# The chunks of a SwiGLU product transposed by DMA on 16-bit halves instead of by TensorE

## What is computed

```python
D_FF = 2816
for l in range(DEPTH):                      # DEPTH = 2
    ...                                     # the mixer: x = x + merged @ w_out[l]
    h2 = rms_norm(x, norm_ffn[l])
    x = x + (jax.nn.silu(h2 @ w_ffn_gate[l]) * (h2 @ w_ffn_up[l])) @ w_ffn_down[l]
```

## Time and profile before

| | |
|---|---|
| median of 3 executions | 848.45 us (848.27 to 849.31) |
| the profiled execution, device time | 849.7 us |
| its span in the profile | 847.9 us |
| granted TensorE clock over the span | 0.999 of full speed |
| PE / DVE / ACT / POOL busy | 842.3 / 552.7 / 420.1 / 69.2 us |

### The profile page before, as it was taken

How to read it: one execution, slowest core, us unless ns; L and a number is a source line. 1 busy time by engine, 2 the same in 40 slices (tenths; PEclk the granted TensorE clock), 3 DMA queues, 4 the chain that set the end, 5 groups by cost and what they waited for, 6 DMA issues and landing times.

```text
span 847.9 us, 10500 instructions
## 1 busy us (share of the span) xinstructions
PE 842.3 (99%) x4100; PEld 689.4 (81%) x4100; DVE 552.7 (65%) x688; ACT 420.1 (50%) x505; POOL 69.2 (8%) x86
## 2 busy tenths in 40 slices
PE   9999999999999999999999999999999999999998
PEld 7888778888888888888888877778888888888886
DVE  5999565657775656654379984565686666656552
ACT  6766544564354444443456665544744544444330
POOL 1333000000030000000024310000000200000000
PEclk9999999999999999999999999999999999999999
DMA  9745334444546555555455543444445555545551
GB/s 351 269 166 192 130 132 174 162 143 157 197 167 226 199 175 175 195 194 187 172 192 199 180 168 106 168 162 148 163 155 194 193 179 192 192 169 186 198 190 59
DMA packets 23116, 151.60 MB, mean 179 GB/s; under 512 B 2816, under 2 KB 2976, under 8 KB 5664
## 3 DMA queue, kind: packets, MB, share of 16 engines
q1 hardware_dynamic: 21152, 144.71, 48.3%
q0 software_dynamic: 1632, 6.18, 2.0%
q10 hardware_dynamic: 288, 0.08, 0.0%
HBM read 149.91 MB, written 1.05 MB: 178 GB/s over the span
## 4 chain that ended last, share of the span: by engine, by line
PE 98%; ACT 1%; DMA 0%; DVE 0%; SPq 0%; issue 0%
PE bank L917 30%; PE bank L919 29%; PE bank L928 29%; PE bank L950 5%; PE bank L1057 2%; PE bank L1033 1%; PE bank L1024 1%; PE bank L997 1%; DMA x_sb<-in_x_dram 0%; PE bank L1003 0%; DVE w_lo L643 0%; PE bank L1067 0%; ACT w_hi L499 0%; ACT zvu L610 0%; ACT aT_hi L509 0%; ACT probsT L521 0%
## 5 line engine op out<-in xcount | busy, mean ns | idle before, releaser
L643 DVE TENSOR_TENSOR w_lo<-w_raw,w_hi 128x2048 fp32r<-128x2048 f32 x134 | 307.0, 2293 | 128.3 <-ACT w_hi L499 128.0
L917 PE MATMUL bank<-w_hi,aT_hi 128*128 128x512 f32 x832 | 333.3, 401 | 0.0
L919 PE MATMUL bank<-w_hi,aT_lo 128*128 128x512 f32 x832 | 325.0, 391 | 0.0
L499 ACT ACTIVATE w_hi<-w_raw 128x2048 fp32r<-128x2048 f32 x134 | 256.1, 1913 | 100.3 <-DMA w_raw<-in_stream_dram 100.1
L928 PE MATMUL bank<-w_lo,aT_hi 128*128 128x512 f32 x832 | 223.7, 391 | 0.1
L917 PEld LDWEIGHTS bank<-w_hi,aT_hi 128*128 128x128 f32 x832 | 156.6, 188 | 36.0 <-issue 5.0
L928 PEld LDWEIGHTS bank<-w_lo,aT_hi 128*128 128x128 f32 x832 | 155.6, 188 | 33.4 <-DVE w_lo L643 0.6
L919 PEld LDWEIGHTS bank<-w_hi,aT_lo 128*128 128x128 f32 x832 | 156.7, 188 | 30.7
L917 PE MATMUL bank<-w_hi,hT_hi 128*128 128x512 f32 x176 | 68.9, 391 | 0.0
L919 PE MATMUL bank<-w_hi,hT_lo 128*128 128x512 f32 x176 | 68.5, 389 | 0.0
L514 ACT ACTIVATE hT_hi<-bank 128x512 fp32r<-128x512 f32 x22 | 13.2, 598 | 78.1 <-PE bank L950 78.1
(11 more groups left out here) (97 smaller groups left out, 717.6 us busy)
## 6 DMA issues: line engine op xcount, KB each, us to landing
w_raw<-in_stream_dram SPq DMA_DIRECT2D x135, 1024.0 KB, 4.7
bias_sb<-in_b_gate_dram POOLq DMA_DIRECT2D x12, 256.0 KB, 4.5
par<-in_params_dram POOLq DMA_DIRECT2D x3, 384.0 KB, 3.5
w_raw<-in_stream_dram SPq DMA_DIRECT2D x4, 256.0 KB, 4.9
pool_mat<-in_pooling_dram POOLq DMA_DIRECT2D x1, 1024.0 KB, 8.2
out_dram<-x_sb SPq DMA_DIRECT2D x4, 256.0 KB, 4.0
x_sb<-in_x_dram SPq DMA_DIRECT2D x2, 256.0 KB, 4.0
x_sb<-in_x_dram SPq DMA_DIRECT2D x1, 512.0 KB, 6.2
```

Source lines behind the costliest of these rows:

```text
L499: nc.scalar.activation(w_hi[:, j % RING, :, :].rearrange("p k n -> p (k n)"), w_raw[:, j % RING, :, :].rearrange("p k n -> p (k n)"), ACT. ...
L643: nc.vector.tensor_tensor(w[0], w[1], w[2].bitcast(F32), ALU.subtract).then_inc(unit_lo, 1)
L917: nc.tensor.matmul(o, src[0][:, k, tok], w_hi[:, slot, wk + i, :], start=first and i == 0, stop=False)
L919: nc.tensor.matmul(o, src[1][:, k, tok], w_hi[:, slot, wk + i, :], start=False, stop=False)
```

## The change

The four PE transposes of each `hid` chunk go, with their PSUM bank. In their place:

- GpSimd, `hidden_halves`: two copies that take the low and the high 16 bits of every float32 of `hid` (all 512 elements of a partition) to `halves`.
- SP, `turn_hidden`: one transposing DMA of 128 x 1024 16-bit elements, `halves` to `turned`, issued right behind the load of a weight unit. Its place is counted from `unit_done`: chunk i is issued when unit `U_FFN` + 2i + 2 is done, and after `halves_ready`. SP's hardware loop over units is written out in Python so that this can stand between two loads.
- GpSimd, `hidden_whole`: two copies that put the halves together again in `hT_raw` (float32, the transposed chunk). GpSimd does halves of i, whole of i, halves of i + 1, and so on.
- ACT and DVE take `hT_hi` and `hT_lo` from `hT_raw` in SBUF, in their step `U_FFN` + 2i + 5, two units later than before. `hT_raw` lies on the memory of `hT_lo`; `halves` and `turned` lie on that of `qkT`.
- PE's matmuls of the down projection wait for `hidden_ready`, which DVE raises.

The PSUM banks 6 and 7 are dealt out to the remaining turns in the same alternation. The diff:

```diff
--- before.py
+++ after.py
@@ -17,6 +17,7 @@
 F32 = mybir.dt.float32
 F32R = mybir.dt.float32r
 BF16 = mybir.dt.bfloat16
+U16 = mybir.dt.uint16
 ALU = mybir.AluOpType
 ACT = mybir.ActivationFunctionType
 AX_X = mybir.AxisListType.X
@@ -124,7 +125,7 @@
     if p is not None:
         out += [("probs", 2 * p), ("probs", 2 * p + 1)]
     out += TURNS_BEFORE.get(t, [])
-    i, odd = divmod(t - U_FFN - 3, 2)
+    i, odd = divmod(t - U_FFN - 5, 2)
     if 0 <= i < FC and not odd:
         out.append(("hidden", i))
     return out
@@ -168,10 +169,9 @@
     n = 0
     for t in range(UNITS):
         for b in turns_before(t) + turns_within(t):
-            if b[0] != "o":
+            if b[0] not in ("o", "hidden"):
                 order[6 + n % 2].append(b)
                 n += 1
-    assert n % 2 == 0
     use = {name: (b, k) for b, names in order.items() for k, name in enumerate(names)}
     return order, use, {b: len(names) for b, names in order.items()}
 
@@ -241,6 +241,11 @@
         x_sb = sb("x_sb", [P, MT, D])
         aT_hi = sb("aT_hi", [P, KT, SEQ], F32R)
         aT_lo = sb("aT_lo", [P, KT, SEQ], F32R)
+        with ExitStack() as shared:
+
+
+            halves = sb("halves", [P, 2, MT, 2, 256], U16, shared)
+            turned = sb("turned", [P, 2, MT, 2, 2, P], U16, shared)
         qkT = sb("qkT", [P, QTILES, SEQ])
         probs = sb("probs", [P, 2, NC])
         probsT = sb("probsT", [P, 2, NC])
@@ -267,6 +272,8 @@
             zvu = sb("zvu", [P, MT, VU_W], F32, mixer)
             gates = sb("gates", [P, MT, 3 * D], F32, mixer)
         hT_hi = sb("hT_hi", [P, KF, SEQ], F32R)
+        with ExitStack() as shared:
+            hT_raw = sb("hT_raw", [P, KF, SEQ], F32, shared)
         hT_lo = sb("hT_lo", [P, KF, SEQ], F32R)
         sg = sb("sg", [P, 2, MT, 256])
         hid = sb("hid", [P, 2, MT, 256])
@@ -314,6 +321,10 @@
         gate_done = sem("gate_done")
         merged_ready = sem("merged_ready")
         sig_done = sem("sig_done")
+        halves_ready = sem("halves_ready")
+        halves_turned = [sem(f"halves_turned{b}") for b in range(2)]
+        raw_ready = sem("raw_ready")
+        hidden_ready = sem("hidden_ready")
         vchain = sem("vchain")
         pchain = sem("pchain")
         out_done = sem("out_done")
@@ -393,13 +404,26 @@
             for s in range(1, RING):
                 sp.dma_start(w_raw[:, s, :, :].rearrange("p k n -> p (k n)"), stream_v[s * P:s * P + P, :]
                              ).then_inc(unit_landed[s], 16)
-            with sp.Fori(1, DEPTH * UNITS // RING) as turn:
-                for s in range(RING):
-
-                    sp.wait_ge(unit_done, turn * RING + (s + 1))
-                    sp.dma_start(w_raw[:, s, :, :].rearrange("p k n -> p (k n)"),
-                                 stream_v[bass.ds((turn * RING + s) * P, P), :]
-                                 ).then_inc(unit_landed[s], 16)
+            def turn_hidden(lay, i):
+
+                n = lay * FC + i
+                sp.wait_ge(halves_ready, 2 * (n + 1))
+                if i >= 2:
+                    sp.wait_ge(raw_ready, 2 * (n - 1))
+                b = i % 2
+                sp.dma_start_transpose(turned[:, b, :, :, :, :].rearrange("p m h k t -> p (m h k) t"),
+                                       halves[:, b, :, :, :].rearrange("p m h f -> p (m h f)")
+                                       ).then_inc(halves_turned[b], 16)
+
+            for u in range(RING, DEPTH * UNITS):
+                s = u % RING
+                sp.wait_ge(unit_done, u + 1)
+                sp.dma_start(w_raw[:, s, :, :].rearrange("p k n -> p (k n)"), stream_v[u * P:u * P + P, :]
+                             ).then_inc(unit_landed[s], 16)
+                lay, t = divmod(u - RING, UNITS)
+                i, odd = divmod(t - U_FFN - 2, 2)
+                if lay >= 0 and 0 <= i < FC and not odd:
+                    turn_hidden(lay, i)
 
             ov = out.rearrange("b (p m) d -> (b p) m d", m=MT)
             for half, first in enumerate(X_BANKS):
@@ -449,6 +473,26 @@
                 pool.dma_start(bias_sb[:, g % 2, :],
                                gate_v[lay * 6 + g:lay * 6 + g + 1, :].to_broadcast([P, NC])
                                ).then_inc(bias_loaded[g % 2], 16)
+
+            def hidden_halves(lay, i):
+
+                b = i % 2
+                for m in range(MT):
+                    wait_emptied(pool, lay, (f"f{i}", m))
+                both = hid[:, b, :, :].bitcast(U16).rearrange("p m (f h) -> p m f h", h=2)
+                for h in range(2):
+                    nc.gpsimd.tensor_copy(halves[:, b, :, h, :], both[:, :, :, h]).then_inc(halves_ready, 1)
+
+            def hidden_whole(lay, i):
+
+                b = i % 2
+                uses = (FC + 1 - b) // 2
+                pool.wait_ge(halves_turned[b], 16 * (lay * uses + i // 2 + 1))
+                both = hT_raw[:, 2 * i:2 * i + 2, :].bitcast(U16).rearrange("p k (m t h) -> p k m t h", m=MT, h=2)
+                for h in range(2):
+                    nc.gpsimd.tensor_copy(both[:, :, :, :, h],
+                                          turned[:, b, :, h, :, :].rearrange("p m k t -> p k m t")
+                                          ).then_inc(raw_ready, 1)
 
             for lay in range(DEPTH):
                 load_bias(lay, 0)
@@ -477,6 +521,9 @@
                 wait_lo(pool, lay, ("ffn_x", 3))
                 load_gains(min(lay + 1, DEPTH - 1))
                 load_params(min(lay + 1, DEPTH - 1))
+                for i in range(FC):
+                    hidden_halves(lay, i)
+                    hidden_whole(lay, i)
 
         @block.scalar
         def _(act):
@@ -507,6 +554,11 @@
                     wait_emptied(act, lay, name)
                     src = scratch[:, NC * (n % 2):NC * (n % 2) + NC]
                     nc.scalar.activation(turn_dest(name, True), turn_view(name, src), ACT.Copy
+                                         ).then_inc(turn_hi, 1)
+                    return
+                if kind == "hidden":
+                    act.wait_ge(raw_ready, 2 * (lay * FC + i + 1))
+                    nc.scalar.activation(turn_dest(name, True), hT_raw[:, 2 * i:2 * i + 2, :], ACT.Copy
                                          ).then_inc(turn_hi, 1)
                     return
                 wait_full(act, lay, name)
@@ -675,6 +727,9 @@
                     src = scratch[:, NC * (k % 2):NC * (k % 2) + NC]
                     nc.vector.tensor_tensor(turn_dest(name, False), turn_view(name, src), hi, ALU.subtract
                                             ).then_inc(turn_lo, 1)
+                elif name[0] == "hidden":
+                    raw = hT_raw[:, 2 * name[1]:2 * name[1] + 2, :]
+                    nc.vector.tensor_tensor(turn_dest(name, False), raw, hi, ALU.subtract).then_inc(hidden_ready, 1)
                 else:
                     ins = nc.vector.tensor_tensor(turn_dest(name, False), turn_view(name, B(name)[:, :]), hi,
                                                   ALU.subtract)
@@ -881,9 +936,13 @@
                         made = []
                         for m in range(MT):
                             dve.wait_ge(sig_done, lay * 2 * FC + (2 * i + m + 1))
+                            if i:
+                                wait_emptied(dve, lay, (f"f{i - 1}", m))
                             made.append(link(nc.vector.scalar_tensor_tensor(
                                 scratch[:, 2 * NC + 256 * m:2 * NC + 256 * m + 256], B((f"f{i}", m))[:, 0:256],
                                 rstd[:, 1, m:m + 1], sg[:, i % 2, m, :], ALU.mult, ALU.mult)))
+                        if i >= 2:
+                            dve.wait_ge(halves_ready, 2 * (lay * FC + i - 1))
                         for m in range(MT):
                             after(lay, made[m])
                             free(nc.vector.scalar_tensor_tensor(
@@ -941,7 +1000,7 @@
 
             def transposes(lay, name):
                 kind, i = name
-                if kind == "o":
+                if kind in ("o", "hidden"):
                     return
                 b = B(name)
                 wait_free(pe, lay, name)
@@ -981,12 +1040,6 @@
 
                         at = 2 * (c % 2) + c // 2 if i < 8 else c
                         last = turn(P * at, probs[:, i % 2, P * c:P * c + P])
-                elif kind == "hidden":
-                    for m in range(MT):
-                        wait_emptied(pe, lay, (f"f{i}", m))
-                    for k in range(2):
-                        for m in range(MT):
-                            last = turn(P * (2 * k + m), hid[:, i % 2, m, P * k:P * k + P])
                 elif kind == "pool":
                     if i == 0:
                         pe.wait_ge(pooling_loaded, 16)
@@ -1116,11 +1169,10 @@
                     else:
                         q = t - U_DOWN
                         if q < 5:
-                            for i in (2 * q, 2 * q + 1):
```

(4 more changed lines are left out.)

## The result

The changed kernel takes 838.04 us (837.88 to 838.81), the kernel before 848.69 in the same comparison: 10.65 us less, ratio 0.987 (95% interval 0.9855 to 0.9884). The forecast was 837.8. The profiled execution took 838.81 us with a span of 837.0, at a granted clock of 1.00.

A forecast was written before the change was run, and what follows sets the result against it. PE, busy 842.3 of 847.9 us, was taken as the bound. Profiled 849.7 us less 22 x 0.48 = 10.6 gives 839.1; 1.25 lower for the median is 837.8 us, range 835.5 to 881 (forecast's own 836 to 841).

The forecast's parts named there:

- PE's share: PE in the FFN: 22 groups of hid transposes removed at 0.48 us each, 10.6 us gained in full.
- PE's busy time: Sign of a right forecast: PE busy 831 to 833 us over the kernel, against 842.3 before.
- The limit T + 18.8: FFN: joined chunk may come 18.8 us after T, start of the unit its transposes stood ahead of, without PE noticing.
- holds under 5.44 us: SP's wait for halves_ready: only the load one unit later stands behind it, so holds up to 5.44 us cost nothing.
- Ready time: FFN round trip: load ahead 3.1, DMA 4.1, copies 1.0, waits 1.2 us; chunk ready at T + 9.4 us.
- D, the transposing DMA: Work of one chunk's 0.26 MB transposing DMA: 2.5 us, bounds 0.8 to 9.5; lands 4.1 us after issue.
- The loop of 8.5 us: GpSimd's halves, DMA and whole in sequence per chunk: 2.1 + 2.3 + 4.1 = 8.5 us, against a 10.88 us period.
- all three fit: FFN: ready time under its limit, GpSimd's loop and DMA engines (8.7 us) within 10.88 us, so added work is hidden.
- Nothing changes for ACT's and DVE's reads: ACT and DVE reading chunks from SBUF instead of PSUM: still 0.60 and 0.69 us a chunk.
- Rival 1: FFN round trip too long: late chunks make ACT hold back weight splits and PE stop; 881 to 925 us, chance 0.24.
- the formula: FFN loss per layer from DMA work D: 10 (D - 4.9), less slack 18.8 - (6.9 + D).
- Rival 2: FFN: GpSimd's copies, sharing time with DVE's two-input work, bind from 1.4 us each; 875 us at 2.0, chance 0.08.

The follow-up runs named there:

- step + 3: The changed kernel with ACT's and DVE's turn of a chunk put back to step U_FFN + 2i + 3: 902.93 us, ratio 1.0643.
- four more: The changed kernel with four more transposing DMAs a chunk, into memory that nothing reads: 878.59 us, ratio 1.0338.

## Why the prediction was right, and where its steps were off

- *PE's share.* 22 groups of 0.48 us, 10.6 us, was the whole of the forecast; 10.65 were measured, and doubling the transposes cost 9.8. Taking start spacings and not the 0.60 us that a group reads (13.2 in all) was the step that mattered. The forecast of PE's busy time, 831 to 833 us, was just missed with 830.0: the busy rows fell by 12.3 us, since they hold part of the overlap.
- *The limit T + 18.8.* Its derivation is borne out by the turn in step + 3, where the limit two units earlier gives 32.6 us a layer against 32.4 measured. At T + 18.8 itself no run reached it as the first limit: in the DMA and copy experiments the weight load held back at SP ran out of time first, at nearly the same lateness (11.1 against 10.7 us). The prediction named that load only for holds under 5.44 us.
- *Ready time.* T + 9.4 forecast, T + 8.1 measured.
- *D, the transposing DMA.* Forecast 2.5 us of work between 0.8 and 9.5; it is 1.3 to 1.6, on the side of the lower bound, where the plain copy of the same bytes makes (0.65 - 0.57) x 120 / 11 = 0.9 us. Alone it lands in 2.7 us, against 4.1. The Trainium skill's 1309 ns for one 128 x 128 block ("VectorE: DVE Perf Modes", The three transpose paths) does not add up over a chunk's eight: all eight land in 2.7 us, fixed time and all. What the Trainium skill says in "Advanced Engine Details and Errata", X-Bar Transpose (TRN2), that such DMAs are as fast as plain ones, is nearer to these traces: the landings agree within 0.3 us, while the DMA engines are busy for 1.6 us and not 0.9.
- *The loop of 8.5 us.* The step that was mis-sized. Copies are 0.61 and 0.76 us and not 0.52, 2.7 a chunk and not 2.1; the waits with DVE are (3.67 - 1.22) = 2.4 us against 2.3. Copies, waits and 2.7 us of DMA make 7.8 us. But I left the weight load ahead of the DMA out of the loop, though the ready time has it, and with it the measured loop is 10.9 us, just the period. By the prediction's own terms it would have been 8.5 + 3.1 = 11.6 us, more than the period, and ten steps would have used 7 of the 9.4 us of slack; the forecast would have stood, but "all three fit" would not. It did no harm, because that part shrinks: with the issue held later, the DMA lands in 2.7 us.
- *Nothing changes for ACT's and DVE's reads.* Wrong in size: DVE's `hT_lo` takes 1.09 us at the median and not 0.69, beside GpSimd's `halves` copies; with the turn in step + 3, where no copy runs beside it, it takes 0.69. DVE had the room.
- *Rival 1.* Its break-even was forecast at D = 6.0 us. With four transposes (5.4 us at 1.34 each) the kernel is still faster than before, with five (6.7 us) it is 30 us slower. The place is right. The price past it was too low: by the formula D = 6.7 gives 863 us, measured 878.6. Its mechanism was half right: ACT did hold back the weight splits, but it waited last for weights that SP had loaded late. Two of its terms were low: the first chunk's true DMA went out 9.4 us later than in the change (267.47 against 258.09) where the formula has 6.7 - 2.5 = 4.2 us, and the ten steps added 20.5 us and not 18.
- *Rival 2.* Forecast to decide at 1.4 us a copy, 5.6 us a chunk. Copies of 2.7 + 4 x 0.61 = 5.1 us are free, 2.7 + 8 x 0.61 = 7.6 us are not. Past that, GpSimd's whole round trip, DVE's hold-ups and the DMA in it, set 13.5 us a chunk, where the rival's shared time alone makes 12.9.
- *A third loop that I did not see.* ACT's wait for chunk i stands ahead of work that chunk i + 1 needs. In the change the turn is two units later, so this loop is open; the prediction weighed only the deadline of the weights, and the expectation from it called step + 3 borderline. It costs 65 us.

## What to carry to other kernels

Where one engine is the bound without gaps, price what leaves it by start to start spacings, and ask of what is added only two things: does each closed loop fit the period, and how late may its result be. Lateness at the last step, less the slack of the deadline, was the loss within 2 us, whether DMAs, copies or a closed loop caused it. Look in each engine's own program for what stands behind a new wait. On SP it was the weight load, which ran out of time before the chunk did. On ScalarE it was the next chunk's sigmoid: a turn one unit too early closed a loop through it and cost six times the gain.

## What the runs showed of the hardware

A transposing DMA of 128 x 1024 16-bit elements from SBUF to SBUF keeps SP for 1.24 us (a plain one 0.47), lands in 2.7 us with nothing ahead of it and 5.8 us behind a 1 MB load, and keeps the DMA engines busy for 1.3 to 1.6 us (an estimate from their shares and from the 12.9 us chunk). Several in a row hold SP: four issues took 5.8 to 9.1 us in the profile with four more. A float32 transpose of 128 x 128 between matmuls costs PE 0.10 us, not the 0.27 of its row. GpSimd's copies and DVE's subtractions of two SBUF operands hold each other up in both directions: 0.61 us became up to 2.8 us for a GpSimd copy, 0.69 became 1.09 us for DVE's subtraction.
